# A three-layer transformer on one core: the last product shared between VectorE and GpSimd, and the output sent in five transfers

## The chip, the cores and the metric

The kernel runs on one core of one Trainium2 chip. The metric is the device time of one execution in microseconds, the median of several runs. Before the change it is 1014.27 us (three runs, 1014.16 to 1014.28).

## What is computed

A token block `x` of 256 tokens by 1024 features goes through three layers (one of `first_block`, two of `second_block`), each a mixer and a gated feed-forward network with a residual. The last step of the reference is the one that the change touches:

```python
def rms_norm_2(x, g):
    xf = x.astype(jnp.float32)
    y = xf * lax.rsqrt(jnp.mean(xf * xf, axis=-1, keepdims=True) + NORM_EPS)
    return (y * g.astype(jnp.float32)).astype(x.dtype)
...
        x = x + (jax.nn.silu(h @ ffn_w_gate[l]) * (h @ ffn_w_up[l])) @ ffn_w_down[l]
    return rms_norm_2(x, final_norm_g)
```

Everything is float32.

## The kernel before

**Layout.** `x` lies in SBUF transposed: 128 partitions by `KT` = 8 tiles of `T` = 256 tokens, so tile k holds features 128k to 128k + 127, and the norm over features is a sum over partitions and tiles. 148 chunks of weights (up to 128 x 2048) are streamed by the SyncE queue into a ring of three buffers, split by ScalarE (`w_hi`) and VectorE (`w_lo`) into two parts, and every product is three matmuls (line 466). The order of the work is written out by hand on each engine. Semaphores tie the engines together: `V`, `A` and `M` count named steps of VectorE, ScalarE and TensorE; `V.at("final", 2)`, for instance, is the count that VectorE reaches with the step marked `final_2`. An engine takes its instructions strictly in the order in which they are written, so a wait holds all that stands behind it on that engine. The DMAs of the output are issued by ScalarE, too.

**The end of the program** is what the change touches. In order of time:

- TensorE ends the last product (`down`, line 466) bank by bank. VectorE adds each pair of tiles to `x` (`residual`, `residual_tile`, line 1658); tile 7 is last.
- ScalarE squares the tiles (lines 1637 and 1641), VectorE sums some of the squares (`part_sum`), and `norm_sum` (lines 505 to 519) sums over the partitions with matmuls against ones.
- Meanwhile VectorE multiplies tiles 0 to 5 of `x` by the gain, into `xg` (line 2379, six instructions, the last marks `final_gain`).
- ScalarE makes the factor `rstd` = (mean + eps)^-0.5 with a logarithm and an exponential (`inverse_root`, lines 1230 and 1232).
- VectorE multiplies tiles 0 and 1, 2 and 3, 4 and 5 of `xg` by `rstd` (line 2384 through `tt`, recorded as line 1658), 128 x 512 each, and then makes tiles 6 and 7 from `x`, gain and factor in one instruction each (line 2386). The steps `final_0` to `final_3` are marked after each pair.
- ScalarE waits for each step and issues the transfer of that pair to `out` (line 1645), 256 KB each. At the end it waits until all four have landed (`stored` reaches 64).

**GpSimd** has little to do: it splits half of the first weight chunk (line 448), and issues two loads of `mat` (line 453) and one of `pos` (line 456), each behind a wait. Its last instruction before is the second load of `mat`, behind the step `mixed_0` of layer 1; then it waits for `mixed_0` of layer 2.

Of the kernel before, what the change touches and what calls it, by code (L numbers as in the profile page):

```python
# [29 lines left out]
ALU = mybir.AluOpType  # L30
# [6 lines left out]
P = 128  # L37
D = 1024
KT = D // P
T = 256  # L40
# [7 lines left out]
LAYERS = 3  # L48
# [178 lines left out]
def program(nc, ins, out, plan):  # L227


    with ExitStack() as ctx:  # L230
        def sb(name, shape, dt=F32):
            return ctx.enter_context(nc.sbuf_tensor(name, shape, dt))

        def sem(name):
            return ctx.enter_context(nc.semaphore(name))


        x = sb("x", [P, KT, T])
# [12 lines left out]
        rstd = sb("rstd", [P, T])  # L251
# [15 lines left out]
        def Par(name, i=None, j=None):  # L267
            a, b = PAR_AT[name]
            return par[:, a:b] if i is None else par[:, a + i:a + (i + 1 if j is None else j)]
# [20 lines left out]
        xg, sq = NORM["xg"], NORM["sq"]  # L290
# [51 lines left out]
        bias_tables = sem("bias_tables_loaded")  # L342
        rel_out, rel_in = sem("bias_row_stored"), sem("bias_hankel_loaded")
        stored = sem("output_stored")
        V = Steps(sem("vector_step"), plan.get("V"))
        A = Steps(sem("scalar_step"), plan.get("A"))
        M = Steps(sem("tensor_step"), plan.get("M"))
# [74 lines left out]
        @block.sync  # L422
        def _(sp):
            sp.dma_start(par[:, :], ins["params"]).then_inc(x_loaded, 16)

            x_in, half = ins["x"].rearrange("p (k t) -> p k t", k=KT), CH // 2
            sp.dma_start(raw[:, 0, 0:half], ins["w"][0, :, 0:half]).then_inc(half_loaded, 16)
            sp.dma_start(x[:, 0:2, :], x_in[:, 0:2, :]).then_inc(x_loaded, 16)
            sp.dma_start(x[:, 2:4, :], x_in[:, 2:4, :]).then_inc(x_more_loaded, 16)
            sp.dma_start(raw[:, 0, half:], ins["w"][0, :, half:]).then_inc(loaded[0], 16)  # L430
            sp.dma_start(x[:, 4:8, :], x_in[:, 4:8, :]).then_inc(x_rest_loaded, 16)
            for c, (l, kind, i, n) in enumerate(STREAM):
                if c == 0:
                    continue
                if c == 2:
                    sp.dma_start(cst[:, 0:NFIRST], ins["consts"][:, 0:NFIRST]).then_inc(tables, 16)
                if c >= RING:

                    split(sp, c - RING)
                sp.dma_start(raw[:, c % RING, 0:n], ins["w"][c, :, 0:n]).then_inc(loaded[c % RING], 16)  # L440
                if c == 3:
                    sp.dma_start(cst[:, NFIRST:], ins["consts"][:, NFIRST:]).then_inc(late_tables, 16)


        @block.gpsimd
        def _(pool):
            pool.wait_ge(half_loaded, 16)
            pool.tensor_scalar(w_hi[:, 0, 0:CH // 2], raw[:, 0, 0:CH // 2], 1.0, 0.0, ALU.mult, ALU.add)\
                .then_inc(hi_pool, 1)
            for l in range(LAYERS):  # L450
                pool.wait_ge(M.sem, M.at(l, "mixed", 0))
                if l + 1 < LAYERS:
                    pool.dma_start(mat[:, 0:NMAT2], ins["mat"][l + 1, :, 0:NMAT2]).then_inc(mats, 16)
                if l == 0:
                    pool.wait_ge(V.sem, V.at(l, "mixed", 3))
                    pool.dma_start(pos, ins["pos"]).then_inc(positions, 16)


        @block.tensor
        def _(pe):  # L460
# [33 lines left out]
            def norm_sum(l, what):  # L494

                into = sum_bank(what)
                if what in ("in", "ffn"):
                    pe.wait_ge(V.sem, V.at(l, what, "sum", 2))
                    if l == 0 and what == "in":
# [7 lines left out]
                if what == "fed":  # L507
                    pe.wait_ge(A.sem, A.at(l, what, "sq", 7))
                    pe.matmul(bank[into][:, 0:T], ONES, sq[:, 7, :], start=False, stop=False)
                    pe.wait_ge(V.sem, V.at(l, what, "part", 3))  # L510
                    pe.matmul(bank[into][:, 0:T], ONES, sq[:, 0, :], start=False, stop=True)\
                        .then_inc(M.sem, M.mark(l, what, "sum"))
                    return
                pe.wait_ge(V.sem, V.at(l, what, "part", 2 if what == "final" else 3))
                pe.matmul(bank[into][:, 0:T], ONES, sq[:, 0, :], start=False, stop=False)
# [6 lines left out]
            def as_they_come(l, what, pieces):  # L522
# [4 lines left out]
                for m in range(KT // n):  # L527
                    pe.wait_ge(V.sem, V.at(l, what, "lo", m))
                    if l == 0 and what == "in":
# [32 lines left out]
            def project(l, *which, between=lambda: None):  # L562

                for i in which:
                    c = CHUNK[l, "in", i]
                    width = STREAM[c][3] // KT
                    if c not in HALVED:
                        split(pe, c)
                    to = projected(l, i)
                    if i >= 3:  # L570
                        pe.wait_ge(V.sem, V.at(l, "in", i - 2))
                    token_major = i in ((3, 9, 11) if l == 0 else (8,))
                    if token_major:
                        s = c % RING
                        for t in range(TT):
                            if t:
                                between()
                            last = product(to[:, t, 0:width],
                                           [lambda k, p=p: p[:, k, t * P:(t + 1) * P] for p in (h_hi, h_lo)],
                                           range(KT),  # L580
                                           [lambda k, p=p: p[:, s, k * width:(k + 1) * width] for p in (w_hi, w_lo)])
                    else:
                        for t, (_, _, at) in enumerate(columns_of(l, i)):
                            if t:
                                between()
                            if c in HALVED and t == 0:
                                first_product(to[:, t, :], c, at)
                            else:
                                last = product(to[:, t, :], tile_of(c, KT, width, at), range(KT), H)
                            if (l, i, t) in ((0, 1, 0), (1, 2, 0), (2, 1, 0)):  # L590
                                norm_sum(l, "in")
                    last.then_inc(M.sem, M.mark(l, "in", i))
# [610 lines left out]
        def _(act):  # L1203
# [78 lines left out]
            def norm_factor(l, what):  # L1282


                if what in ("in", "ffn") and (l, what) not in BY_TILE[1:]:
                    ln_and_exp()
                act.wait_ge(M.sem, M.at(l, what, "sum"))
                inverse_root(rstd[:, :], bank[sum_bank(what)][:, 0:T], 1.0 / D, Mc("eps"), (l, what, "rstd"))
# [351 lines left out]
                act.wait_ge(V.sem, V.at(2, "fed_tile", k))  # L1640
                act.activation(sq[:, k, :], x[:, k, :], ACT.Square).then_inc(A.sem, A.mark(LAYERS, "final", "sq", k))
            norm_factor(LAYERS, "final")
            for m in range(4):
                act.wait_ge(V.sem, V.at("final", m))
                act.dma_start(out[:, 2 * m * T:2 * (m + 1) * T],
                              xg[:, 2 * m:2 * m + 2, :].rearrange("p k t -> p (k t)"))\
                    .then_inc(stored, 16)
            act.wait_ge(stored, 64)


        @block.vector
        def _(dve):
            def wide(v, n):

                return v.unsqueeze(1).broadcast_to([P, n, v.shape[-1]])

            def tt(dst, a, b, op, *name):
                ins_ = dve.tensor_tensor(dst, a, b, op)  # L1658
                if name:
                    ins_.then_inc(V.sem, V.mark(*name))  # L1660
                return ins_

            def after_v(*name):
                dve.wait_ge(V.sem, V.at(*name))
# [713 lines left out]
            for k in range(6):  # L2378
                last = dve.tensor_scalar(xg[:, k, :], x[:, k, :], Par("final", k), None, ALU.mult)
            last.then_inc(V.sem, V.mark("final_gain"))  # L2380
            after_a(LAYERS, "final", "rstd")
            after_v("final_gain")
            for m in range(3):
                tt(xg[:, 2 * m:2 * m + 2, :], xg[:, 2 * m:2 * m + 2, :], wide(rstd[:, :], 2), ALU.mult, "final", m)
            for k in (6, 7):
                last = dve.scalar_tensor_tensor(xg[:, k, :], x[:, k, :], Par("final", k), rstd[:, :],
                                                ALU.mult, ALU.mult)
            last.then_inc(V.sem, V.mark("final", 3))

    return {"V": V.log, "A": A.log, "M": M.log}  # L2390

# [102 lines left out]
```

## Time and profile before

| what | us |
|---|---|
| median of three runs | 1014.27 |
| time of the profiled execution | 1013.86 |
| its span, first to last instruction | 1012.1 |
| TensorE busy in it | 996.9 |
| VectorE busy | 684.5 |
| ScalarE busy | 501.2 |
| GpSimd busy | 3.0 |

The profiled execution's time is 1.76 us longer than its span (what lies before the first and behind the last instruction) and 0.41 us below the median. The granted clock of TensorE is 0.999 of full speed. Names in the rows: PE is TensorE, DVE is VectorE, ACT is ScalarE, POOL is GpSimd, and a q behind a name is its queue or sequencer. `arena` is the large SBUF buffer in which `xg` and `sq` lie. Two instructions of one engine can overlap by some 0.1 us in the rows, since the next one starts while the last one's results drain.

### The profile page before, as it was taken

The page shows a single profiled execution, that of the slowest core. Times are in us where ns is not written, and L with a number is a line of the kernel's source. Part 1 is how long each engine was busy: PE and PEld are TensorE (multiplying, and loading weights), DVE is VectorE, ACT ScalarE, POOL GpSimd, SP SyncE. Part 2 cuts the span into 40 slices and gives each one's busy share as a digit, 9 for nine tenths or more (in the row PEclk, how much of TensorE's full clock was granted, in tenths as well). Part 3 has the DMA queues.
Part 4 walks back from the last instruction along what each step waited for, and adds up shares of the span by engine and source line. Part 5 has one row for each costly group of instructions (what it writes and reads, how often), then busy time and mean ns, then how long its engine had stood idle before and what let it go on. Part 6 is the DMA issues. An engine that isn't in the chain of part 4 may idle for free.

```text
span 1012.1 us, 20189 instructions
## 1 busy us (share of the span) xinstructions
PE 996.9 (98%) x8762; PEld 948.7 (94%) x8762; DVE 684.5 (68%) x1093; ACT 501.2 (50%) x667; POOL 3.0 (0%) x8
## 2 busy tenths in 40 slices
PE   9999999999999999999999999999999999999997
PEld 8898999999999889889999999999887999999997
DVE  6868586785656897856665565588877566565555
ACT  6466664435345652645544434375436364434433
POOL 0000000000000000000000000000000000000000
PEclk9999999999999999999999999999999999999999
DMA  9535345455544332314454545543231254555531
GB/s 332 179 113 200 138 147 190 173 209 186 189 170 159 109 111 85 124 46 141 167 208 174 196 173 180 196 161 116 79 111 44 89 203 170 189 184 173 202 126 42
DMA packets 24024, 156.41 MB, mean 155 GB/s; under 512 B 2608, under 2 KB 3936, under 8 KB 6400
## 3 DMA queue, kind: packets, MB, share of 16 engines
q1 hardware_dynamic: 21888, 151.70, 41.7%
q10 hardware_dynamic: 1840, 2.50, 0.7%
q8 instruction: 69, 1.13, 0.4%
q0 software_dynamic: 208, 0.92, 0.3%
q14 instruction: 19, 0.16, 0.0%
HBM read 154.05 MB, written 1.06 MB: 153 GB/s over the span
## 4 chain that ended last, share of the span: by engine, by line
PE 87%; DVE 6%; ACT 3%; issue 2%; DMA 1%; SPq 0%; ACTq 0%; DVEq 0%
PE bank L466 73%; DVE w_lo L1676 2%; ACT w_hi L1207 2%; DVE arena L1658 1%; PE bank L921 1%; PE bank L926 1%; PE bank L937 1%; DVE x L1658 1%; DMA x<-in_x 1%; PE bank L1145 1%; PE bank L1175 1%; DVE arena L2150 1%; DVE h_lo L1690 0%; ACT h_hi L1251 0%; PE bank L884 0%
## 5 line engine op out<-in xcount | busy, mean ns | idle before, releaser
L466 PE MATMUL bank<-h_hi,w_hi 128*128 128x256 f32 x1480 | 424.3, 287 | 3.7 <-DVE arena L1770 1.5
L1676 DVE TENSOR_TENSOR w_lo<-raw,w_hi 128x2048 fp32r<-128x2048 f32 (+2 forms) x142 | 318.7, 2250 | 155.9 <-ACT w_hi L1207 155.3
L466 PE MATMUL bank<-h_lo,w_hi 128*128 128x256 f32 x1480 | 418.7, 283 | 0.0
L466 PE MATMUL bank<-h_hi,w_lo 128*128 128x256 f32 x1480 | 418.6, 283 | 0.0
L1207 ACT ACTIVATE w_hi<-raw 128x2048 fp32r<-128x2048 f32 (+2 forms) x151 | 271.3, 1801 | 77.1 <-PE bank L466 74.9
L466 PEld LDWEIGHTS bank<-h_hi,w_hi 128*128 128x128 f32 x1480 | 283.6, 192 | 11.0 <-issue 4.9
L466 PEld LDWEIGHTS bank<-h_lo,w_hi 128*128 128x128 f32 x1480 | 283.7, 192 | 1.0 <-issue 0.7
L466 PEld LDWEIGHTS bank<-h_hi,w_lo 128*128 128x128 f32 x1480 | 283.7, 192 | 0.0
L466 PE MATMUL bank<-mix_hi,w_hi 128*128 128x256 f32 x720 | 207.0, 287 | 2.2 <-DVE mix_lo L1658 1.4
L466 PE MATMUL bank<-mix_lo,w_hi 128*128 128x256 f32 x720 | 203.7, 283 | 0.0
L466 PE MATMUL bank<-mix_hi,w_lo 128*128 128x256 f32 x720 | 203.7, 283 | 0.0
L466 PEld LDWEIGHTS bank<-mix_hi,w_hi 128*128 128x128 f32 x720 | 138.1, 192 | 5.1 <-DVE mix_lo L1658 2.3
L466 PEld LDWEIGHTS bank<-mix_lo,w_hi 128*128 128x128 f32 x720 | 138.1, 192 | 1.0 <-issue 1.0
L466 PEld LDWEIGHTS bank<-mix_hi,w_lo 128*128 128x128 f32 x720 | 138.1, 192 | 0.0
L1321 ACT ACTIVATE arena<-arena 128x256 f32<-128x256 f32 x66 | 27.6, 418 | 194.9 <-DVE arena L1658 194.9
L1658 DVE TENSOR_TENSOR arena<-arena 128x256 f32<-128x256 f32 (+2 forms) x134 | 71.6, 541 | 47.5 <-ACT arena L1321 35.3
L1207 ACT ACTIVATE arena<-bank 128x256 f32<-128x256 f32 (+3 forms) x72 | 30.9, 448 | 49.8 <-PE bank L603 17.2
L1658 DVE TENSOR_TENSOR mix_lo<-arena,mix_hi 128x256 fp32r<-128x256 f32 (+1 forms) x70 | 30.8, 441 | 33.3 <-ACT mix_hi L1207 33.3
L1207 ACT ACTIVATE mix_hi<-arena 128x256 fp32r<-128x256 f32 (+1 forms) x70 | 30.1, 430 | 38.5 <-DVE arena L1658 37.3
L1658 DVE TENSOR_TENSOR arena<-bank,rstd 128x512 f32<-128x512 f32 x66 | 45.1, 684 | 0.0
L466 PE MATMUL bank<-w_hi,h_hi 128*128 128x256 f32 (+1 forms) x84 | 25.7, 306 | 0.0
L1258 ACT ACTIVATE h_hi<-x,par 128x256 fp32r<-128x256 f32 x32 | 14.1, 500 | 22.6 <-DVE x L1658 16.5
(310 smaller groups left out, 844.3 us busy)
## 6 DMA issues: line engine op xcount, KB each, us to landing
raw<-in_w SPq DMA_DIRECT2D x136, 1024.0 KB, 4.8
raw<-in_w SPq DMA_DIRECT2D x5, 512.0 KB, 3.9
raw<-in_w SPq DMA_DIRECT2D x2, 896.0 KB, 4.4
raw<-in_w SPq DMA_DIRECT2D x2, 768.0 KB, 4.7
cst<-in_consts SPq DMA_DIRECT2D x1, 1184.0 KB, 10.6
arena<-bias_rows ACTq DMA_DIRECT2D x1, 1024.0 KB, 7.3
out<-arena ACTq DMA_DIRECT2D x4, 256.0 KB, 2.1
mat<-in_mat POOLq DMA_DIRECT2D x2, 384.0 KB, 3.4
```

The lines of the kernel that those rows point to most:

```text
L466: last = pe.matmul(dst, w[a](k), act[b](k), start=start and i == 0 and j == 0, stop=stop and i == n - 1 and j == 2, skip_group_check=loose)
L921: last = pe.matmul(blocks(quads(2 + q)[h, m % 4, 0:64], n, 1), Y[h, m, :], blocks(XT[h, m, :], n, 1), start=True, stop=True)
L926: last = pe.matmul(blocks(quads(q)[h, m % 4, 0:64], n, 0), XT[h, m, :], blocks(Y[h, m, :], n, 0), start=True, stop=True)
L937: last = pe.matmul(quads(q)[h, m % 4, 0:64], BT[h, m, :], Xm[h, m, :], start=True, stop=True)
L1145: pe.matmul(dst(i), AT2["qn"][:, i - 4, queries], AT2["kn"][:, i - 4, keys], start=True, stop=False)
L1175: pe.matmul(dst(j), value(j, 0), att_p(l, j)[:, 0:T], start=True, stop=False)
L1207: return act.activation(dst, src, ACT.Copy, **kw)
L1258: last = act.activation(h_hi[:, k, :], x[:, k, :], ACT.Copy, scale=Par(g, k))
L1321: act.activation(FF["sg"][:, j % 2, :], FF["gu"][:, j % 2, 0, :], ACT.Silu)\
L1658: ins_ = dve.tensor_tensor(dst, a, b, op)
L1676: dve.tensor_tensor(w_lo[:, s, 0:n], raw[:, s, 0:n], w_hi[:, s, 0:n].bitcast(F32), ALU.subtract)\
L2150: last = dve.copy_predicated(gram[:, g, 2 * n:2 * n + 2, :].rearrange("p a b -> p (a b)"), mask, pairs(g % 4)[:, n, :])
```

## The change

VectorE multiplies only two pairs of `xg` by the factor (tiles 0 to 3); GpSimd does the pair 4 and 5, with one 128 x 512 product behind waits for `final_gain` and `rstd`, and reports on a semaphore of its own. VectorE's tiles 6 and 7 each mark a step. ScalarE issues five transfers in the order 0-1, 2-3, 6, 4-5, 7. What is computed is the same.

```diff
@@ -342,6 +342,7 @@
         bias_tables = sem("bias_tables_loaded")
         rel_out, rel_in = sem("bias_row_stored"), sem("bias_hankel_loaded")
         stored = sem("output_stored")
+        scaled_pool = sem("output_tiles_scaled_by_gpsimd")
         V = Steps(sem("vector_step"), plan.get("V"))
         A = Steps(sem("scalar_step"), plan.get("A"))
         M = Steps(sem("tensor_step"), plan.get("M"))
@@ -454,6 +455,10 @@
                 if l == 0:
                     pool.wait_ge(V.sem, V.at(l, "mixed", 3))
                     pool.dma_start(pos, ins["pos"]).then_inc(positions, 16)
+            pool.wait_ge(V.sem, V.at("final_gain"))
+            pool.wait_ge(A.sem, A.at(LAYERS, "final", "rstd"))
+            pool.tensor_tensor(xg[:, 4:6, :], xg[:, 4:6, :], rstd[:, :].unsqueeze(1).broadcast_to([P, 2, T]), ALU.mult)\
+                .then_inc(scaled_pool, 1)
 
 
         @block.tensor
@@ -1640,12 +1645,12 @@
                 act.wait_ge(V.sem, V.at(2, "fed_tile", k))
                 act.activation(sq[:, k, :], x[:, k, :], ACT.Square).then_inc(A.sem, A.mark(LAYERS, "final", "sq", k))
             norm_factor(LAYERS, "final")
-            for m in range(4):
-                act.wait_ge(V.sem, V.at("final", m))
-                act.dma_start(out[:, 2 * m * T:2 * (m + 1) * T],
-                              xg[:, 2 * m:2 * m + 2, :].rearrange("p k t -> p (k t)"))\
+
+            for k, n, done in ((0, 2, 0), (2, 2, 1), (6, 1, 2), (4, 2, None), (7, 1, 3)):
+                act.wait_ge(scaled_pool, 1) if done is None else act.wait_ge(V.sem, V.at("final", done))
+                act.dma_start(out[:, k * T:(k + n) * T], xg[:, k:k + n, :].rearrange("p k t -> p (k t)"))\
                     .then_inc(stored, 16)
-            act.wait_ge(stored, 64)
+            act.wait_ge(stored, 80)
 
 
         @block.vector
@@ -2380,12 +2385,11 @@
             last.then_inc(V.sem, V.mark("final_gain"))
             after_a(LAYERS, "final", "rstd")
             after_v("final_gain")
-            for m in range(3):
+            for m in range(2):
                 tt(xg[:, 2 * m:2 * m + 2, :], xg[:, 2 * m:2 * m + 2, :], wide(rstd[:, :], 2), ALU.mult, "final", m)
             for k in (6, 7):
-                last = dve.scalar_tensor_tensor(xg[:, k, :], x[:, k, :], Par("final", k), rstd[:, :],
-                                                ALU.mult, ALU.mult)
-            last.then_inc(V.sem, V.mark("final", 3))
+                dve.scalar_tensor_tensor(xg[:, k, :], x[:, k, :], Par("final", k), rstd[:, :], ALU.mult, ALU.mult)\
+                    .then_inc(V.sem, V.mark("final", k - 4))
 
     return {"V": V.log, "A": A.log, "M": M.log}
 
```

How this moves instructions, at the end of three engines. First VectorE, from the gains on, before:

```order
L2379 TENSOR_SCALAR arena<-x,par 128x256 x6
L1658 TENSOR_TENSOR arena<-arena,rstd 128x512 [waits vector_step,scalar_step]
L1658 TENSOR_TENSOR arena<-arena,rstd 128x512 x2
L2386 SCALAR_TENSOR_TENSOR arena<-x,par,rstd 128x256 x2
L230 UNCONDITIONAL_BRANCH
```

and after the change:

```order
L2384 TENSOR_SCALAR arena<-x,par 128x256 x6
L1663 TENSOR_TENSOR arena<-arena,rstd 128x512 [waits vector_step,scalar_step]
L1663 TENSOR_TENSOR arena<-arena,rstd 128x512
L2391 SCALAR_TENSOR_TENSOR arena<-x,par,rstd 128x256 x2
L230 UNCONDITIONAL_BRANCH
```

One of the three products with the factor has left VectorE. It stands now at the end of GpSimd (before, the branch was all that followed the second load of `mat`):

```order
L449 TENSOR_SCALAR w_hi<-raw 128x1024 [waits half_of_first_chunk_loaded]
L454 DMA mat<-in_mat 128x768 [waits tensor_step]
L457 DMA arena<-in_pos 128x256 [waits vector_step]
L454 DMA mat<-in_mat 128x768 [waits tensor_step]
L460 TENSOR_TENSOR arena<-arena,rstd 128x512 [waits scalar_step,vector_step,tensor_step]
L230 UNCONDITIONAL_BRANCH
```

Nothing stands behind the product on GpSimd. Then ScalarE, which makes the factor and issues the output, before:

```order
L1230 ACTIVATE rstd<-bank5,cst 128x256 [waits tensor_step]
L1232 ACTIVATE rstd<-rstd 128x256 [waits scalar_step]
L1645 DMA out<-arena 128x512 [waits vector_step] x4
L230 UNCONDITIONAL_BRANCH [waits output_stored]
```

and after the change:

```order
L1235 ACTIVATE rstd<-bank5,cst 128x256 [waits tensor_step]
L1237 ACTIVATE rstd<-rstd 128x256 [waits scalar_step]
L1651 DMA out<-arena 128x512 [waits vector_step] x2
L1651 DMA out<-arena 128x256 [waits vector_step]
L1651 DMA out<-arena 128x512 [waits output_tiles_scaled_by_gpsimd]
L1651 DMA out<-arena 128x256 [waits vector_step]
L230 UNCONDITIONAL_BRANCH [waits output_stored]
```

The issue of tile 7 stands behind the wait for GpSimd. SyncE and TensorE keep their instructions.

## Rows read from the trace of the kernel before

**Rows 1.** Page: busy us by engine; the chain that ended last, by engine and line

```profile
PE 996.9 (98%) x8762; PEld 948.7 (94%) x8762; DVE 684.5 (68%) x1093; ACT 501.2 (50%) x667; POOL 3.0 (0%) x8
...
PE 87%; DVE 6%; ACT 3%; issue 2%; DMA 1%; SPq 0%; ACTq 0%; DVEq 0%
PE bank L466 73%; DVE w_lo L1676 2%; ACT w_hi L1207 2%; DVE arena L1658 1%; PE bank L921 1%; PE bank L926 1%; PE bank L937 1%; DVE x L1658 1%; DMA x<-in_x 1%; PE bank L1145 1%; PE bank L1175 1%; DVE arena L2150 1%; DVE h_lo L1690 0%; ACT h_hi L1251 0%; PE bank L884 0%
```

**Rows 2.** Chain of waits, last stretch, in order of time: start us, us, what

```profile
1004.05 0.59 PE bank L506 x2
1004.64 0.43 PE bank L515 x2
1005.07 0.43 PE bank L517 x2
1005.50 0.45 PE bank L519 x2
1005.95 0.02 issue
1005.97 0.48 ACT rstd L1230
1006.46 0.02 issue
1006.48 0.42 ACT rstd L1232
1006.90 0.02 issue
1006.93 0.69 DVE arena L1658
1007.62 0.60 DVEq L230
1008.22 0.60 DVE arena L1658
1008.82 0.79 DVE arena L2386 x2
```

**Rows 3.** Timeline of DVE, last stretch: start us, us, engine line op, count, idle before

```profile
1004.43 1.66 DVE L2379 TENSOR_SCALAR arena<-x,par 128x256 f32<-128x256 f32 x6
...
1006.93 1.90 DVE L1658 TENSOR_TENSOR arena<-arena,rstd 128x512 f32<-128x512 f32 x3 [0.84 <-ACT rstd L1232]
...
1007.53 0.68 DVE L1658 TENSOR_TENSOR arena<-arena,rstd 128x512 f32<-128x512 f32 x1
...
1008.14 0.69 DVE L1658 TENSOR_TENSOR arena<-arena,rstd 128x512 f32<-128x512 f32 x1
...
1008.74 0.48 DVE L2386 SCALAR_TENSOR_TENSOR arena<-x,par,rstd 128x256 f32<-128x256 f32 x1
...
1009.13 0.48 DVE L2386 SCALAR_TENSOR_TENSOR arena<-x,par,rstd 128x256 f32<-128x256 f32 x1
```

**Rows 4.** Timeline of the ACT queue: the four issues of the output

```profile
1007.65 0.37 ACTq L1645 DMA_DIRECT2D out<-arena  x1
...
1008.25 0.35 ACTq L1645 DMA_DIRECT2D out<-arena  x1
...
1008.86 0.34 ACTq L1645 DMA_DIRECT2D out<-arena  x1
...
1009.65 0.34 ACTq L1645 DMA_DIRECT2D out<-arena  x1
```

**Rows 5.** Busy time by stretch; DMA share and GB/s are the last columns

```profile
core 0: us, PE busy (x) PEld busy (x) DVE busy (x) ACT busy (x) POOL busy (x), PEclk, DMA share, GB/s
...
1008.40:1008.50 0.10, 0.00 (x0) 0.00 (x0) 0.10 (x1) 0.00 (x0) 0.00 (x0) 1.00 0.00 0
1008.50:1010.40 1.90, 0.00 (x0) 0.00 (x0) 1.11 (x3) 0.00 (x0) 0.00 (x0) 0.81 1.04 401
1010.40:1010.60 0.20, 0.00 (x0) 0.00 (x0) 0.00 (x0) 0.00 (x0) 0.00 (x0) 0.50 0.71 267
1010.60:1011.20 0.60, 0.00 (x0) 0.00 (x0) 0.00 (x0) 0.00 (x0) 0.00 (x0) 0.50 0.99 386
1011.20:1011.30 0.10, 0.00 (x0) 0.00 (x0) 0.00 (x0) 0.00 (x0) 0.00 (x0) 0.50 0.10 21
1011.30:1012.10 0.80, 0.00 (x0) 0.00 (x0) 0.00 (x0) 0.00 (x0) 0.00 (x0) 0.50 0.00 0
```

**Rows 6.** The four output DMAs: time of an issue, and from issue to landing

```profile
L1645 ACTq DMA_DIRECT2D out<-arena x4: 338/345/368, 1007.7 to 1009.6; - x4
...
DMA to landing us min/median/max: 2.0/2.1/2.2
```

**Rows 7.** Timeline of POOL, the whole execution after its constants

```profile
5.75 1.04 POOL L448 TENSOR_SCALAR w_hi<-raw 128x1024 fp32r<-128x1024 f32 x1 [5.30 <-DMA raw<-in_w]
114.36 0.71 POOL L453 DMA_DIRECT2D mat<-in_mat  x1 [107.57 <-PE bank L466]
132.58 0.54 POOL L456 DMA_DIRECT2D arena<-in_pos  x1 [17.51 <-DVE x L1658]
461.67 0.54 POOL L453 DMA_DIRECT2D mat<-in_mat  x1 [328.56 <-PE bank L466]
```

**Rows 8.** Two instructions that make an engine ready: POOL at the start, ACT before the end

```profile
L448 POOLq MODIFY_POOL_CONFIG  x2: 11/11/11, 0.7 to 0.8; - x2
...
L1269 ACT ACT_TABLE_LOAD  x1: 1283/1283/1283, 995.6 to 995.6; - x1
```

## The prediction

> **What bounds the kernel now.** I read the page first [rows 1]: TensorE is busy for 98% of the span and is 87% of the chain that ended last. The change touches nothing of that. TensorE's last product is over before the stretch in question, so only the chain's tail counts, and I follow it in order of time [rows 2]: four pairs of matmuls for the norm end at 1005.95, ScalarE makes the factor until 1006.90, and VectorE starts its final products at 1006.93. From there to the end of the span (1012.10) are 5.17 us, and no engine but VectorE, ScalarE's queue and the DMA engines has work in it. That is all this change can move.
>
> The chain says that VectorE is on the path until 1009.61, and here one view misleads. VectorE's timeline [rows 3] gives starts at 1006.93, 1007.53 and 1008.14 for the three 128 x 512 products (0.60 us apart, each about 0.69 long) and at 1008.74 and 1009.13 for tiles 6 and 7 (0.39 apart, 0.48 long). The issues follow each ready pair by 0.03 to 0.04 us [rows 4]. But the busy time by stretch [rows 5] shows what the DMA engines do meanwhile: nothing until 1008.50, then 401 GB/s with a share of 1.04, that is, full, until 1010.40; a small dip (267 GB/s) until 1010.60; again 386 until 1011.20, and silence from 1011.30. The output is one MB, and the DMA engines carry it almost without a pause. Three of the four transfers queue behind each other's bytes; VectorE is only just ahead of them.
>
> From these rows comes a small model. The first issue at 1007.65 puts data on the move at 1008.52 (between the empty stretch and the full one): 0.87 us. A transfer of 256 KB takes 262,144 B / 401 GB/s = 0.65 us, one of 128 KB 0.33. The last data is followed by 0.9 us to the end of the span. The model on the kernel before: data of the four at 1008.52, 1009.17, 1009.82 and, since the issue of 1009.65 arrives only at 1010.52, a pause of 0.05, then until 1011.17. The rows say 1011.2. Its sum 1011.17 + 0.9 is 0.03 short of the span. The landings, 2.0 to 2.2 us after the issue [rows 6], hold the same parts: 0.87 and 0.65 and a return.
>
> **The change, part by part.**
>
> *A product leaves VectorE.* One pitch of 0.60 us goes: tiles 0-1 and 2-3 as before, tile 6 starts at 1008.14 and ends at 1008.62, tile 7 ends at 1009.01 instead of 1009.61. VectorE is done 0.60 us earlier.
>
> *Two issues become three.* An issue takes 0.34 to 0.37 us of ScalarE's queue [rows 6]. None is seen back to back there; I add 0.04 between two and use 0.39. With one more, the queue has five: 1007.65, 1008.25, 1008.65 (tile 6), then 4-5 at 1009.04 if GpSimd is ready, then tile 7 at 1009.43. The last leaves 0.22 us earlier than before.
>
> *The product on GpSimd.* The trace has no such instruction. The nearest row is GpSimd's one piece of arithmetic [rows 7]: 128 x 1024 with one input in 1.04 us. Half as many elements at the same rate is the low end, 0.52 us; the upper end is twice the row, 2.08, if a second input costs as much again and a short instruction carries a large fixed part. I take 1.04: 512 elements of each of two inputs are as many reads as that row's 1024. The Trainium skill (GPSIMD Engine Reference, section "Elementwise — side-by-side cycle accounting") gives 4497 ns for a two-input product of 2048 elements; a quarter of it, an estimate, is 1.12 us before any fixed part, and the sum would come out the same by it.
>
> *The new wait.* ScalarE now waits for GpSimd with one thing queued behind it, tile 7's issue; nobody else waits for either. Started at 1006.93 beside VectorE, GpSimd would be done at 1007.97, and tiles 4-5 are wanted only at 1009.04. It could take up to 2.3 us (until 1009.25) before the DMA engines ran dry, because the data in front of tiles 4-5 (0.65 + 0.65 + 0.33 us from 1008.52) lasts until 1010.15 and an issue needs 0.03 + 0.87 to reach it. That is above my upper end, so the cost is nothing; the cover is the queue of earlier bytes, and if it is gone each later us is a us.
>
> *The sum.* Data starts at 1008.52 as before, since the first pair is untouched, and flows without a pause for 3 x 0.65 + 2 x 0.33 = 2.61 us, until 1011.13. The model had 1011.17 before. So of VectorE's 0.60 us only the pause is gained, 0.04 us, and nothing is gained by the smaller last transfer, because it is last in one stream of the same bytes. 1013.86 - 0.04 = 1013.82 for the profiled execution, which lies 0.41 below the median; on the median 1014.23, rounded **1014.2 us**. The two added semaphore steps and one added issue lie beside this stream.
>
> **The rivals.**
>
> *A. One after the other.* Every final instruction of VectorE reads two large operands from SBUF, and GpSimd's new one reads two as well, released by the same step. If they cannot read at once, 1.04 us of GpSimd is added to VectorE's 2.08. GpSimd first: all of VectorE moves by 1.04, the first issue is at 1008.69, data starts at 1009.56 and ends 2.61 later at 1012.17, that is +1.00. GpSimd after the first product: the model gives the end at 1012.21, +1.04. GpSimd last, from 1009.01: done 1010.05, tiles 4-5 issued at 1010.08, their data from 1010.95 to 1011.60, tile 7's until 1011.93, +0.76. I take +1.0: 1015.2. With GpSimd's bounds it is +0.2 (0.52 us, last) to +2.1 (2.08 us, between). For it: nothing in the trace excludes it. Against it: nothing in the trace shows it either, since GpSimd's arithmetic at 5.75 ends at 6.79 [rows 7] and has no two-input work of VectorE beside it. The Trainium skill (SBUF — State Buffer, section "Who interferes with whom") speaks for this rival: a VectorE instruction with two SBUF inputs contends with a GpSimd instruction that reads SBUF, and the later one blocks fully. By that rule the sum is this rival's, not mine.
>
> *B. The last issue decides.* If the end followed the last issue and its own size instead of the stream, it would be 0.22 + 0.33 = 0.55 us earlier: 1013.7. The full DMA share [rows 5] is against it.
>
> *C. GpSimd comes too late, slower by more than 0.2%.* (0.2%, 2.03 us, is about what a measurement of this kernel can tell from no change.) Its product is its first two-input instruction and its first work since 461.67 [rows 7]. The place is ScalarE's wait, the price is GpSimd's end: last data = that end + 0.03 + 0.87 + 0.65 + 0.33. For +2.03 it must be done after 1011.32, 4.4 us behind the factor. Getting ready at the price of ScalarE's table load (1.28 us, [rows 8]), its own upper end of 2.08, and VectorE's 2.08 in front of it make 5.44, so 1012.37: +3.1, 1017.3. Against it: before its first arithmetic GpSimd's two pool configurations took 11 ns each at 0.7 to 0.8 [rows 8], and the split came out as soon as its half chunk had landed, so no such start-up is seen; and three mishaps would have to meet unless one is very large.
>
> That the change doesn't do what it says: the orders of the engines show the product on GpSimd and the five issues, so only its effect is open. If GpSimd's wait were released late by ScalarE's step, that is rival C.
>
> **How the numbers follow.** Forecast, both engines side by side: 0.50, since each engine in these rows keeps its own duration beside others. Rival A: 0.40, B: 0.04, C and the top of A: 0.06. The range goes from 1013.9 (the forecast less 0.3 for the spread between median and profile and a part of B) to 1015.9 (A with GpSimd at about 1.7 us); it holds the forecast and nearly all of A. The forecast's own range is 1013.9 to 1014.5. Within 0.2%: all of the forecast, B, and A but for its top, 0.93. Slower by over 0.2%: 0.06. Faster by over 0.2%: 0.01; even 5.17 us hold no mechanism for it, for factor to first data (1.6) and last data to end (0.9) stay, and so does the 2.61 of bytes.
>
> **What would show it.** In the profile after: VectorE's last instruction ends near 1009.0, 0.60 earlier relative to the factor, and its two products still start 0.60 apart (rival A: one gap of about a us in or before them, or GpSimd's row starting late or stretched to 3 us). GpSimd's row is about 1 us and over before tile 6's issue. Five issues, the last three 0.39 apart; with C or the last form of A a gap before the fourth. The DMA share stays full from the first byte to the last, with no dip, for 2.6 us. The forecast is wrong if the dip persists while the issues are early, if the end moves with VectorE's 0.60 us, or if the first product's step comes later than 0.69 us behind its start.

## The result

The changed kernel takes 1015.49 us (median of 22 runs, 1015.04 to 1015.77), the kernel before 1014.19 (22 runs, 1013.66 to 1014.39). The ratio is 1.0013, with a 95% interval of 1.0007 to 1.0019: slower by 1.3 us. That is less than the 0.2% by which the chances of the prediction were cut, but the interval lies wholly above 1, so the kernel is slower. The forecast was 1014.2, the range 1013.9 to 1015.9; what came is rival A, in its form "GpSimd after the first product".

The profiled execution of the change took 1015.51 us, its span is 1013.7. Of the 1.6 us more than before, 0.39 arose before the stretch that was changed: the factor was ready at 1007.29, and at 1006.90 before [rows 2]. Over all profiled runs of this study VectorE's first product with the factor starts between 1006.93 and 1007.49, with the same instructions ahead of it on TensorE, VectorE and ScalarE. So what follows is read from that start: to the end of the span it was 1012.1 - 1006.93 = 5.17 us before, and is 1013.7 - 1007.32 = 6.38 now, 1.2 us more.

The chain of waits of the changed kernel, from the factor on, in order of time (start us, us, what), which answers to the end of [rows 2]:

```profile
1006.87 0.43 ACT rstd L1237
1007.29 0.02 issue
1007.32 0.69 DVE arena L1663
1008.01 1.67 DVEq L230
1009.67 0.79 DVE arena L2391 x2
```

Where the chain had two pieces of 0.60 behind the first product, it has one of 1.67. What it is shows the timeline of VectorE (start us, us, engine line op, count, idle before), which answers to [rows 3]:

```profile
1007.32 0.69 DVE L1663 TENSOR_TENSOR arena<-arena,rstd 128x512 f32<-128x512 f32 x1 [0.84 <-ACT rstd L1237]
...
1007.92 1.75 DVE L1663 TENSOR_TENSOR arena<-arena,rstd 128x512 f32<-128x512 f32 x1
...
1009.60 0.47 DVE L2391 SCALAR_TENSOR_TENSOR arena<-x,par,rstd 128x256 f32<-128x256 f32 x1
...
1009.99 0.47 DVE L2391 SCALAR_TENSOR_TENSOR arena<-x,par,rstd 128x256 f32<-128x256 f32 x1
```

The second product starts 0.60 us behind the first as before, but takes 1.75 us in place of 0.69. The first one keeps its 0.69, and tiles 6 and 7 take 0.47 each (0.48 before). GpSimd's timeline has what stood beside it:

```profile
1007.46 1.67 POOL L460 TENSOR_TENSOR arena<-arena,rstd 128x512 f32<-128x512 f32 x1 [544.89 <-ACT rstd L1237]
```

GpSimd starts at 1007.46, 0.14 behind VectorE's first product, and ends at 1009.13. VectorE's second product ends 0.54 later, at 1009.67. VectorE's first product ends at 1008.01 (1007.32 + 0.69), 1.12 us before GpSimd is done. The two engines took turns: VectorE's first, GpSimd's, VectorE's second. The rows show the order; that it is the reads from SBUF that exclude each other is shown by e3 and e5 below. The five issues of the output, on the ACT queue, answer to [rows 4]:

```profile
1008.04 0.37 ACTq L1651 DMA_DIRECT2D out<-arena  x1
...
1009.71 0.35 ACTq L1651 DMA_DIRECT2D out<-arena  x1
...
1010.10 0.44 ACTq L1651 DMA_DIRECT2D out<-arena  x1
...
1010.58 0.98 ACTq L1651 DMA_DIRECT2D out<-arena  x2
...
1011.10 0.46 ACTq L1651 DMA_DIRECT2D out<-arena  x1
```

The second issue follows VectorE's second product, 1.67 us behind the first issue (0.60 before). The wait for GpSimd itself held nothing: tiles 4-5 had been ready since 1009.13 when they were issued at 1010.58, behind tile 6. The busy time by stretch answers to [rows 5] (the last two columns are the DMA share and GB/s):

```profile
core 0: us, PE busy (x) PEld busy (x) DVE busy (x) ACT busy (x) POOL busy (x), PEclk, DMA share, GB/s
1008.90:1009.60 0.70, 0.00 (x0) 0.00 (x0) 0.70 (x2) 0.00 (x0) 0.23 (x1) 1.00 0.95 372
1009.70:1010.50 0.80, 0.00 (x0) 0.00 (x0) 0.77 (x2) 0.00 (x0) 0.00 (x0) 0.66 0.00 0
1010.50:1012.60 2.10, 0.00 (x0) 0.00 (x0) 0.00 (x0) 0.00 (x0) 0.00 (x0) 0.50 0.99 370
1012.60:1012.70 0.10, 0.00 (x0) 0.00 (x0) 0.00 (x0) 0.00 (x0) 0.00 (x0) 0.50 0.30 92
1012.80:1013.70 0.90, 0.00 (x0) 0.00 (x0) 0.00 (x0) 0.00 (x0) 0.00 (x0) 0.50 0.00 0
```

The first transfer's bytes flow for 0.7 us, then the DMA engines are empty from 1009.70 to 1010.50, then full until 1012.60. The last byte is 5.38 us behind VectorE's start (the stretch that ends at 1012.70), and was 4.37 before (the one that ends at 1011.30): 1.0 us. These stretches are 0.1 us wide, and so is the uncertainty of every "last byte" here. The last 0.2 us of the 1.2 lie behind it: from the last byte to the end of the span 1.0 us instead of 0.8.

### The profile page after: what moved, and what is told of

Its sections match the earlier page's. It is cut to its first block, busy times and chain, and to the rows that moved or that the text cites. A ratio compares the mean times of both kernels' runs of the same rounds, so it can differ in the third digit from the quotient of the medians.

```text
span 1013.7 us, 20190 instructions
## 1 busy us (share of the span) xinstructions
PE 996.8 (98%) x8762; PEld 948.6 (94%) x8762; DVE 685.0 (68%) x1092; ACT 501.9 (50%) x667; POOL 4.7 (0%) x9
## 4 chain that ended last, share of the span: by engine, by line
PE 87%; DVE 6%; ACT 3%; issue 2%; DMA 1%; SPq 0%; DVEq 0%; ACTq 0%
PE bank L471 73%; DVE w_lo L1681 2%; ACT w_hi L1212 2%; DVE arena L1663 1%; PE bank L926 1%; PE bank L931 1%; PE bank L942 1%; DVE x L1663 1%; DMA x<-in_x 1%; PE bank L1150 1%; PE bank L1180 1%; DVE arena L2155 1%; DVE h_lo L1695 0%; ACT h_hi L1256 0%; PE bank L889 0%
```

## The experiments

The times of e1 to e9 are medians of 11 runs, with the kernel before beside them on the same chip (33 runs for e1 to e8, 15 for e9; the chip is not the same for all experiments, which is why the number beside them differs). The theory was S: GpSimd's product and VectorE's products exclude each other at their reads from SBUF, and the second loses the whole time of the first. Its main rivals were T (the fifth transfer and the slower issues) and W (any work of GpSimd holds VectorE). From VectorE's start to the end and to the last byte is read from the profiles.

| kernel | median us, before beside it | ratio, 95% interval | second product us | last byte us | end us |
|---|---|---|---|---|---|
| before | | | 0.68 | 4.37 | 5.17 |
| the change | 1015.49, 1014.19 | 1.0013 (1.0007 to 1.0019) | 1.75 | 5.38 | 6.38 |
| e1: five transfers, GpSimd idle | 1014.40, 1014.22 | 1.0002 (0.9994 to 1.0011) | not stretched | 4.39 | 5.39 |
| e2: GpSimd's share, four transfers | 1015.09, 1014.22 | 1.0010 (1.0001 to 1.0019) | 1.75 | 5.34 | 6.14 |
| e3: GpSimd with one input | 1014.68, 1014.22 | 1.0006 (0.9997 to 1.0015) | 1.10 | 4.75 | 5.75 |
| e4: GpSimd only writes | 1014.28, 1014.12 | 1.0002 (0.9993 to 1.0011) | not stretched | 4.39 | 5.39 |
| e5: factor in PSUM for VectorE | 1014.28, 1014.22 | 1.0003 (0.9994 to 1.0011) | not stretched | 4.39 | 5.29 |
| e6: GpSimd last | 1015.05, 1014.12 | 1.0009 (1.0000 to 1.0018) | not stretched | 5.11 | 5.91 |
| e7: single tiles, two queues | 1014.26, 1014.12 | 1.0002 (0.9993 to 1.0011) | single tiles | 4.21 | 5.21 |
| e8: e5 with four transfers | 1014.11, 1014.12 | 1.0000 (0.9991 to 1.0009) | not stretched | 4.30 | 5.10 |
| e9: five transfers, pair last | 1014.35, 1013.96 | 1.0003 (0.9994 to 1.0012) | not stretched | 4.57 | 5.37 |

The last column, less 5.17, and the difference of the medians agree within 0.2 us throughout. Of the experiments only e2's ratio has an interval wholly above 1 (e6's starts at 1.0000); for the others no difference in the median is shown, and what is said of their parts rests on one profile each.

**e1, the split of the output alone.** Against the change:

```diff
-            for k, n, done in ((0, 2, 0), (2, 2, 1), (6, 1, 2), (4, 2, None), (7, 1, 3)):
+            for k, n, done in ((0, 2, 0), (2, 2, 1), (4, 2, 2), (6, 1, 3), (7, 1, 4)):
...
-            for m in range(2):
+            for m in range(3):
                 tt(xg[:, 2 * m:2 * m + 2, :], xg[:, 2 * m:2 * m + 2, :], wide(rstd[:, :], 2), ALU.mult, "final", m)
```

and without GpSimd's waits and product.

> The split of the output alone: VectorE makes all three products as before, GpSimd none; five transfers 0-1, 2-3, 4-5, 6, 7. Theory S (GpSimd's product and VectorE's products exclude each other at their reads): no cost is left, VectorE's steps are 0.60 us apart, the stream of output bytes stays closed, 1014.2 us (the kernel before: 1014.19). Rival T (the fifth transfer and the slower issues back to back, 0.48 instead of 0.39 us, are the loss): 1015.4. Rival V (VectorE is the path, as the chain of waits says): the smaller last transfer gives 0.3 us, 1013.9.

1014.40 us: T is out as the main cause. The stream of bytes, by stretch:

```profile
core 0: us, PE busy (x) PEld busy (x) DVE busy (x) ACT busy (x) POOL busy (x), PEclk, DMA share, GB/s
1009.00:1011.60 2.60, 0.00 (x0) 0.00 (x0) 1.10 (x3) 0.00 (x0) 0.00 (x0) 0.92 1.04 394
1011.60:1011.80 0.20, 0.00 (x0) 0.00 (x0) 0.00 (x0) 0.00 (x0) 0.00 (x0) 0.50 0.39 123
1011.80:1012.80 1.00, 0.00 (x0) 0.00 (x0) 0.00 (x0) 0.00 (x0) 0.00 (x0) 0.50 0.00 0
```

It is full until it ends, 4.39 us behind VectorE's start at 1007.41, as in the kernel before. V is out too: the smaller last transfer did not bring the end forward. But the last row shows 1.0 us from the last byte to the end, where it was 0.8; I come back to that in e9.

**e2, GpSimd's share alone.**

```diff
-            for k, n, done in ((0, 2, 0), (2, 2, 1), (6, 1, 2), (4, 2, None), (7, 1, 3)):
+            for k, n, done in ((0, 2, 0), (2, 2, 1), (4, 2, None), (6, 2, 3)):
```

> The share of GpSimd alone: tiles 4-5 on GpSimd, but four transfers 0-1, 2-3, 4-5, 6-7. Theory S: VectorE's second product stretched to about 1.75 us as in the change, 1015.4 us. Rival T: 1014.2.

1015.09 us, 0.87 above the kernel before: S by its mechanism, 0.3 less than it said. The timeline of GpSimd and VectorE:

```profile
1007.30 1.66 POOL L460 TENSOR_TENSOR arena<-arena,rstd 128x512 f32<-128x512 f32 x1 [544.86 <-ACT rstd L1237]
...
1007.77 1.75 DVE L1663 TENSOR_TENSOR arena<-arena,rstd 128x512 f32<-128x512 f32 x1
```

The picture of the change again: GpSimd ends at 1008.96, VectorE's second product 0.56 later. The last byte is at 5.34 as in the change (5.38), and the return is 0.8 instead of 1.0. Loss by the share: some 0.9 to 1.0 us; loss by five transfers with a lone last tile: some 0.2. In the profiles the two add up (0.97 in e2 and 0.22 in e1, against 1.21 in the change); in the medians 0.25 us is left over (0.87 and 0.18, against 1.30), which is within the intervals.

**e3, GpSimd with one input.** Tiles 4 and 5 are copied in place, without the factor, so this kernel leaves out a part of the result:

```diff
-            pool.tensor_tensor(xg[:, 4:6, :], xg[:, 4:6, :], rstd[:, :].unsqueeze(1).broadcast_to([P, 2, T]), ALU.mult)\
+            pool.tensor_scalar(xg[:, 4:6, :], xg[:, 4:6, :], 1.0, 0.0, ALU.mult, ALU.add)\
                 .then_inc(scaled_pool, 1)
```

> The change with GpSimd's product replaced by a one-input operation on the same tiles (times 1.0; the factor is left out of tiles 4 and 5). Theory S, any read of GpSimd excludes VectorE's second input: GpSimd's instruction is shorter (about 0.6 us alone, from 1.04 us for twice the size), VectorE's second product is still stretched, by 0.5 to 0.6 us, 1014.8. Theory S2, only two inputs on both sides exclude each other: VectorE's pitch 0.60 us, 1014.2.

1014.68 us. The timeline:

```profile
1007.13 0.99 POOL L460 TENSOR_SCALAR arena<-arena 128x512 f32<-128x512 f32 x1 [544.91 <-ACT rstd L1237]
...
1007.56 1.10 DVE L1663 TENSOR_TENSOR arena<-arena,rstd 128x512 f32<-128x512 f32 x1
```

S2 is out. So is the thought that the two engines collide because both read the factor: GpSimd does not read it here. A GpSimd instruction that reads one operand holds VectorE's second product as well: it takes 1.10 us, and ends 0.54 behind GpSimd's end (1008.12), the same 0.54 as in the change. In both, the long one and the short one, VectorE's product ends about 0.54 us behind GpSimd's end. The stretch is 0.42 us, below the 0.5 to 0.6 expected: once VectorE's first product is over (1007.64), GpSimd needs only 0.48 more.

**e4, GpSimd writes only.** Tiles 4 and 5 are filled with zeros, so their result is left out:

```diff
-            pool.tensor_tensor(xg[:, 4:6, :], xg[:, 4:6, :], rstd[:, :].unsqueeze(1).broadcast_to([P, 2, T]), ALU.mult)\
-                .then_inc(scaled_pool, 1)
+            pool.memset(xg[:, 4:6, :], 0.0).then_inc(scaled_pool, 1)
```

> The change with GpSimd's product replaced by a memset of tiles 4 and 5 (their result is left out). Theory S (it is the reads that exclude each other): VectorE's steps 0.60 us apart, the last byte 4.4 us behind VectorE's start, 1014.2. Rival W (GpSimd's writes hold VectorE, too): the second product stretched by 0.3 us or more, 1014.6 or more.

1014.28 us. The timeline:

```profile
1007.21 1.29 DVE L1662 TENSOR_TENSOR arena<-arena,rstd 128x512 f32<-128x512 f32 x2 [0.84 <-ACT rstd L1236]
...
1007.33 0.52 POOL L460 MEMSET arena<- 128x512 f32 x1 [544.83 <-ACT rstd L1236]
```

GpSimd's 0.52 us lie inside VectorE's first product (until 1007.90), and the pair of products takes 1.29 us, unstretched. By its median it would be S. But the memset ended (1007.85) just as VectorE's second product began (0.60 behind the first, 1007.81), so this run shows that GpSimd's writes do not lengthen VectorE's first product; it says nothing on a second one queued behind a longer write. No run has this memset alone, so whether its 0.52 us hold a wait can only be estimated. In the change GpSimd's own 1.26 us (measured in e6), counted back from its end, begin 0.55 us behind VectorE's start. A memset held until then would have had 0.09 us left here, and even a memset of 128 x 1 takes 0.10 at the start of this trace. By that estimate it was not held. W is weakened, and e5 decides it.

**e5, VectorE's factor in PSUM.** The logarithm as before, then two exponentials, and VectorE reads `bank[4]`:

```diff
+            act.activation(bank[4][:, 0:T], rstd[:, :], ACT.Exp, scale=-0.5).then_inc(A.sem, A.mark(LAYERS, "final", "rstd"))
+            act.activation(rstd[:, :], rstd[:, :], ACT.Exp, scale=-0.5).then_inc(A.sem, A.mark(LAYERS, "final", "rstd_copy"))
...
-                tt(xg[:, 2 * m:2 * m + 2, :], xg[:, 2 * m:2 * m + 2, :], wide(rstd[:, :], 2), ALU.mult, "final", m)
+                tt(xg[:, 2 * m:2 * m + 2, :], xg[:, 2 * m:2 * m + 2, :], wide(bank[4][:, 0:T], 2), ALU.mult, "final", m)
```

Tiles 6 and 7 read the same bank, and GpSimd waits for `rstd_copy`.

> The change, but ScalarE writes the factor to PSUM first, for VectorE, and 0.45 us later a copy to SBUF, for GpSimd; so VectorE's products have one input in SBUF and GpSimd's two. Theory S: no stretching on either side, GpSimd's product about 1.1 us, VectorE done 0.60 us earlier than before, and the stream of bytes closed: 1014.2. If the stream were not the bound: 1013.8. Rival W (any work of GpSimd holds VectorE): 1015.4 as in the change.

1014.28 us. The timeline of both engines:

```profile
1007.11 1.29 DVE L1668 TENSOR_TENSOR arena<-arena,bank 128x512 f32<-128x512 f32 x2 [0.81 <-ACT bank L1651]
...
1007.59 1.26 POOL L460 TENSOR_TENSOR arena<-arena,rstd 128x512 f32<-128x512 f32 x1 [545.19 <-ACT rstd L1652]
...
1008.31 0.47 DVE L2396 SCALAR_TENSOR_TENSOR arena<-x,par,bank 128x256 f32<-128x256 f32 x1
```

Here GpSimd runs from 1007.59 to 1008.85 beside VectorE's two products and tile 6, and neither waits: VectorE's pair takes 1.29 us, tile 6 starts at 1008.31, and GpSimd's product takes 1.26 instead of 1.67. What was taken away is VectorE's second read from SBUF. GpSimd's start also moved, to 0.48 us behind VectorE's first product from 0.14, but its product still overlaps VectorE's first for 0.21 us and the whole of the second. Both engines still read and write `arena`, so sharing the buffer is not the cause. W is out, and S stands on VectorE's side: what matters is whether it reads two operands from SBUF. On GpSimd's side a read is enough (e3); that a write alone is harmless rests on e4 and its estimate. And yet nothing is won, as the busy time by stretch shows:

```profile
core 0: us, PE busy (x) PEld busy (x) DVE busy (x) ACT busy (x) POOL busy (x), PEclk, DMA share, GB/s
1008.60:1008.70 0.10, 0.00 (x0) 0.00 (x0) 0.10 (x1) 0.00 (x0) 0.10 (x1) 1.00 0.00 0
1008.70:1011.30 2.60, 0.00 (x0) 0.00 (x0) 0.48 (x2) 0.00 (x0) 0.15 (x1) 0.96 1.05 395
1011.30:1011.50 0.20, 0.00 (x0) 0.00 (x0) 0.00 (x0) 0.00 (x0) 0.00 (x0) 0.50 0.35 108
1011.60:1012.40 0.80, 0.00 (x0) 0.00 (x0) 0.00 (x0) 0.00 (x0) 0.00 (x0) 0.50 0.00 0
```

VectorE is done 0.6 us earlier than in the kernel before (2.06 us behind its start, against 2.68), and the last byte leaves 4.39 us behind its start, against 4.37. The DMA engines are full for 2.6 us without a gap, from 1008.70 on.

**e6, GpSimd last.**

```diff
-            pool.wait_ge(V.sem, V.at("final_gain"))
+            pool.wait_ge(V.sem, V.at("final", 3))
...
-            for k, n, done in ((0, 2, 0), (2, 2, 1), (6, 1, 2), (4, 2, None), (7, 1, 3)):
+            for k, n, done in ((0, 2, 0), (2, 2, 1), (6, 1, 2), (7, 1, 3), (4, 2, None)):
```

> GpSimd's product only after VectorE's last one, transfer 4-5 sent last: its duration alone. Beside VectorE's one-input work it took 1.26 us, in the change 1.67. Theory S: alone 1.2 to 1.3 us, VectorE's steps 0.60 us apart; GpSimd starts about 2.2 us behind VectorE's start and ends at 3.5, issue, 0.87 to the data and 0.65 of data: last byte 5.05 behind VectorE's start against 4.37 before: 1014.9. Rival R (GpSimd's product is simply slow, 1.67 us whatever stands beside it): 1015.3.

1015.05 us. The timeline:

```profile
1007.49 1.29 DVE L1663 TENSOR_TENSOR arena<-arena,rstd 128x512 f32<-128x512 f32 x2 [0.84 <-ACT rstd L1237]
...
1008.70 0.88 DVE L2391 SCALAR_TENSOR_TENSOR arena<-x,par,rstd 128x256 f32<-128x256 f32 x2
...
1009.72 1.26 POOL L460 TENSOR_TENSOR arena<-arena,rstd 128x512 f32<-128x512 f32 x1 [546.93 <-DVE arena L2391]
```

Alone, GpSimd's product takes 1.26 us, the same as beside VectorE's one-input work in e5, so R is out: its 1.67 us in the change are 0.41 longer, and the explanation that fits is a wait for VectorE's first product. The last byte at 5.11 was expected at 5.05.

**e7 and e8, two tries at a version that beats both.** e8 is e5 with e2's four transfers:

```diff
-            for k, n, done in ((0, 2, 0), (2, 2, 1), (6, 1, 2), (4, 2, None), (7, 1, 3)):
+            for k, n, done in ((0, 2, 0), (2, 2, 1), (4, 2, None), (6, 2, 3)):
```

e7 is e5 with tiles 0 to 3 as four single products and transfers:

```diff
+            for k, n, done in ((1, 1, 1), (3, 1, 3), (4, 2, None)):
+                sp.wait_ge(scaled_pool, 1) if done is None else sp.wait_ge(V.sem, V.at("final", done))
+                sp.dma_start(out[:, k * T:(k + n) * T], xg[:, k:k + n, :].rearrange("p k t -> p (k t)"))\
+                    .then_inc(stored, 16)
...
-            for k, n, done in ((0, 2, 0), (2, 2, 1), (6, 1, 2), (4, 2, None), (7, 1, 3)):
+            for k, n, done in ((0, 1, 0), (2, 1, 2), (6, 1, 4), (7, 1, 5)):
```

> An attempt to move the bound itself: factor in PSUM for VectorE, tiles 0 to 3 as single products and single transfers, shared between ScalarE's and SyncE's queues, 4-5 by GpSimd, 6 and 7 single. If the stream of bytes is the bound, only an earlier first byte helps: tile 0 is ready 0.42 instead of 0.69 us behind the factor, first byte 1.3 instead of 1.57, then the bytes of 1 MB; rows of 1 KB may slow them to 0.36 us for 128 KB: last byte 4.2 to 4.3, 1014.1. If issues or VectorE are the bound: 1013.8 or less.

> The factor in PSUM for VectorE, GpSimd's product at its own pace, and four transfers 0-1, 2-3, 4-5, 6-7 in place of five. Theory S with the stream as bound: as the kernel before or 0.05 us less, 1014.1 to 1014.2; tiles 4-5 are ready 1.75 us behind VectorE's start, so the bytes follow each other closely and end at 4.2 to 4.3. If VectorE's 0.6 us counted: 1013.6.

e7 took 1014.26 us and e8 1014.11, with 1014.12 for the kernel before. The bytes of e7 by stretch:

```profile
core 0: us, PE busy (x) PEld busy (x) DVE busy (x) ACT busy (x) POOL busy (x), PEclk, DMA share, GB/s
1008.50:1008.60 0.10, 0.00 (x0) 0.00 (x0) 0.10 (x1) 0.00 (x0) 0.10 (x1) 1.00 0.00 0
1008.60:1011.40 2.80, 0.00 (x0) 0.00 (x0) 0.88 (x3) 0.00 (x0) 0.43 (x1) 0.83 1.05 373
1011.40:1011.60 0.20, 0.00 (x0) 0.00 (x0) 0.00 (x0) 0.00 (x0) 0.00 (x0) 0.50 0.10 26
```

VectorE starts at 1007.29 in it, so the first byte comes 1.3 us behind that start instead of 1.57, and the last at 4.21 instead of 4.37: the end of the stream follows its beginning, as the model says, and the part of the earlier start that is missing went into the rate: 373 GB/s here, where all transfers but that of tiles 4-5 have rows of 1 KB per partition, and 401 before with rows of 2 KB. Whether the row size or the second queue does this was not separated. 0.16 us is no difference that the medians show, and the return behind the lone last tile takes it back. e8 has the shortest way to the end in its profile (5.10 against 5.17), and its median is that of the kernel before. Neither beats it measurably.

**e9, the pair last.** e1 with one line changed:

```diff
-            for k, n, done in ((0, 2, 0), (2, 2, 1), (4, 2, 2), (6, 1, 3), (7, 1, 4)):
+            for k, n, done in ((0, 2, 0), (2, 2, 1), (4, 1, 2), (5, 1, 2), (6, 2, 4)):
```

> Five transfers as in the split of the output alone, all by VectorE, but 0-1, 2-3, 4, 5, 6-7: the pair is last, not tile 7. In the runs so far the span ended 0.8 us behind the last byte where a transfer of 256 KB was last (the kernel before, two of the experiments with four transfers, and GpSimd last with five), and 0.9 to 1.0 where tile 7 alone was last. Theory L (the lone last tile costs this 0.1 to 0.2 us): from VectorE's start to the end 5.2 us as in the kernel before. Rival F (the fifth transfer costs it, wherever it stands): 5.4 us as in the split alone. In the median both lie within 0.2 us of 1014.2, which the runs can hardly tell; the profile decides.

5.37 us from VectorE's start to the end: the number that rival F gave. But the parts are not F's. The bytes by stretch:

```profile
core 0: us, PE busy (x) PEld busy (x) DVE busy (x) ACT busy (x) POOL busy (x), PEclk, DMA share, GB/s
1008.50:1010.50 2.00, 0.00 (x0) 0.00 (x0) 1.11 (x3) 0.00 (x0) 0.00 (x0) 0.58 0.98 370
1010.50:1010.80 0.30, 0.00 (x0) 0.00 (x0) 0.00 (x0) 0.00 (x0) 0.00 (x0) 0.50 0.59 205
1010.80:1011.40 0.60, 0.00 (x0) 0.00 (x0) 0.00 (x0) 0.00 (x0) 0.00 (x0) 0.50 1.02 399
1011.40:1011.50 0.10, 0.00 (x0) 0.00 (x0) 0.00 (x0) 0.00 (x0) 0.00 (x0) 0.50 0.27 82
1011.50:1012.30 0.80, 0.00 (x0) 0.00 (x0) 0.00 (x0) 0.00 (x0) 0.00 (x0) 0.50 0.00 0
```

The return is back at 0.8 us, as theory L has it. What took its place stands between 1010.50 and 1010.80, a dip to 205 GB/s. Its cause is in the ACT queue, the issues of tile 5 and of the pair:

```profile
1009.23 0.47 ACTq L1647 DMA_DIRECT2D out<-arena  x1
...
1009.75 0.47 ACTq L1647 DMA_DIRECT2D out<-arena  x1
```

The pair was ready at 1009.61 (VectorE's steps are those of [rows 3] here) and is issued at 1009.75, since the issue of tile 5 ahead of it starts at 1009.23 and takes 0.47 us. By the model that later issue (2.82 us behind VectorE's start, 2.72 before) is worth 0.10 of the 0.20 by which the last byte is late; the other 0.10 is not assigned, and the rate up to 1010.50, 370 GB/s with two lone tiles in it against 401 before, is a candidate. So the run is undecided as it was put: the return goes with the size of the last transfer, as L has it, but the fifth transfer costs some 0.2 us by another way, and all of this is one profile. The return, from the last byte to the end, is 0.8 in the five kernels where a transfer of 256 KB is last (before, e2, e6, e8, e9) and 0.9 to 1.0 in the six where tile 7 is (the change, e1, e3, e4, e5, e7). Why a smaller last transfer returns later stays open.

## Why the prediction was wrong

- **The step that failed** is in "The product on GpSimd" and "The new wait": "Started at 1006.93 beside VectorE, GpSimd would be done at 1007.97", with the reason in the chances that "each engine in these rows keeps its own duration beside others". No row showed GpSimd's arithmetic beside a VectorE instruction with two SBUF inputs, and the prediction said so, yet gave the side-by-side case 0.50 against 0.40. e5 and e6 give the measured price: 1.26 us for GpSimd's product when nothing holds it; in the change it waits 0.4 us for VectorE, and then holds VectorE for 1.07 us (1.75 less 0.68).
- **Rival A** named the mechanism and the order. It gave the last byte +1.04 us; measured +1.01. Two errors nearly cancel in it, which is luck: GpSimd was sized at 1.04 us, and 1.12 of it lie behind VectorE's first product; and VectorE's second product, already started, needs 0.54 us after GpSimd's end, where a whole 0.69 was counted. The rule of the Trainium skill that the prediction set beside it (SBUF — State Buffer, section "Who interferes with whom") is borne out in each of its halves that ran: two SBUF inputs against a read of GpSimd, the later one blocked until the first ends (the change, e2, e3), and no contention with one SBUF input (e5). The part on a GpSimd that only writes is not tested beyond the estimate in e4. Rival A should have had the larger chance, since no row spoke against it.
- **The size of GpSimd's product** was 1.04 us within 0.52 to 2.08; it is 1.26. The estimate from the Trainium skill (GPSIMD Engine Reference, section "Elementwise — side-by-side cycle accounting"), 1.12 us before any fixed part, is near that; the page's 4497 ns are for an addition of two inputs, not a product.
- **The output as a stream of bytes was right**, and it is why VectorE's 0.60 us are worth nothing: with the contention away (e5) VectorE is done early, and the last byte stays at 4.39. Rival B, the last issue decides, is out by e1 and e5. The 0.04 us of gain was not seen; in e1, e4 and e5 the last byte is at 4.39 against 4.37.
- **Two issues become three** was undersized: an issue right behind another took 0.44 to 0.47 us in the change, with starts 0.48 to 0.52 apart, for the 0.39 assumed from one start to the next. It costs nothing under a full stream, and some 0.1 us where it stands before the last transfer (e9).
- **The last 0.2 us** had no term: the return behind a lone last tile was taken to be that of the kernel before (0.9 us in the model, whose last byte is at 1011.17; 0.8 from the 1011.30 used here).
- **Rival C**, GpSimd too late, did not come: it starts 0.14 us behind VectorE's first product after 545 us of idleness, with no start-up.

In sum, for the profile: +1.0 us at the last byte, most of it the 0.8 us and more in which the DMA engines are empty while VectorE waits for GpSimd, and +0.2 of return, against a forecast of -0.04.

## What to carry to other kernels

Before an elementwise product is shared between VectorE and GpSimd, look at where the operands of both lie: in this kernel, with both reading SBUF and VectorE reading two operands there, the two took turns, and most of GpSimd's time was added to the chain. Putting VectorE's common operand into PSUM took this away here for the price of a second 0.4 us activation. And before an engine at the end of a chain is relieved, look at the DMA share behind it: where the bytes already flowed without a gap, an engine that was done 0.6 us earlier (e5) brought nothing. An earlier first byte brought the last one forward by 0.16 us in the profile of e7; fewer bytes were not tried.

## What the runs showed of the hardware that was not expected

- VectorE's blocked product shows as one long instruction: its start is recorded at its usual place, 0.60 us behind the previous one, and the whole wait lies inside its 1.75 us. Neither the list of waits nor its idle time shows it; the chain has it as one piece of 1.67 us of VectorE's queue.
- The time left to it after GpSimd's end is nearly the same for a long and a short GpSimd instruction: 0.54 us in the change, 0.56 in e2, 0.54 in e3.
- In these runs an issue of the output on the ACT queue took 0.34 to 0.37 us when the queue had been free, and 0.44 to 0.48 right behind another (0.48 in e2, 0.47 at most in the change, e1 and e9).
- From the last byte to the end of the span: 0.8 us behind a transfer of 256 KB (five kernels), 0.9 to 1.0 behind one of 128 KB (six), each from one profile. The cause is open.
